# Compressed attention scores: from eight small matmuls in each query block to one set in each layer, turned per block

## The reference, cut to what matters

```python
k_c = rotary(compress(k_cmp, cmp_w1_k, cmp_w2_k), cmp_end, ROPE_DIM, ROPE_THETA)
v_c = compress(v_cmp, cmp_w1_v, cmp_w2_v)
mask_c = cmp_end[None, :] <= pos[:, None]
s_c = jnp.einsum('bsgjd,bngd->bgjsn', q, k_c)
p_c = masked_softmax(s_c, mask_c) * mask_c
o_cmp = jnp.einsum('bgjsn,bngd->bsgjd', p_c.astype(v_c.dtype), v_c)
...
o = g[..., 0:1] * o_cmp + g[..., 1:2] * o_slc + g[..., 2:3] * o_win
```

## Time and profile before

| | |
|---|---|
| median of 3 executions | 2146.18 us (2144.44 to 2149.34) |
| profiled execution, its own time | 2142.9 us |
| its span in the profile | 2141.1 us |
| PE busy | 2087.1 us, 97% of the span, 9868 instructions |
| DVE busy | 1229.9 us, 57% |
| ACT / POOL busy | 670.5 us / 918.6 us |
| granted TensorE clock, mean | 0.99 of full speed |

### The profile page before, as it was taken

One profiled execution on the slowest core, in us unless ns is written; L12 is line 12 of the kernel. 1 busy time (PEld: TensorE's weight loads), 2 busy tenths in 40 slices (PEclk: granted clock), 3 DMA queues, 4 the chain that ended last, 5 costly groups with the idle time before them and its releaser, 6 DMA issues.

```text
span 2141.1 us, 32149 instructions
## 1 busy us (share of the span) xinstructions
PE 2087.1 (97%) x9868; PEld 1646.9 (77%) x9868; DVE 1229.9 (57%) x1849; ACT 670.5 (31%) x977; POOL 918.6 (43%) x672
## 2 busy tenths in 40 slices
PE   8999999999999999999999999899999999999997
PEld 6766666788888788888877666668888887888886
DVE  8666767523235888872257668665223278888522
ACT  4244523333332322222223444223233322222222
POOL 3422224444445555545544222234444455555553
PEclk9999999999999999999999999999999999999998
DMA  5311123223232222223232111222322222222323
GB/s 195 104 58 40 50 64 99 80 97 98 98 98 92 96 93 94 97 91 118 95 116 93 50 43 48 82 84 86 102 94 97 98 99 89 98 98 93 107 98 108
DMA packets 57275, 194.90 MB, mean 91 GB/s; under 512 B 6880, under 2 KB 7392, under 8 KB 57056
## 3 DMA queue, kind: packets, MB, share of 16 engines
q1 hardware_dynamic: 52416, 186.14, 25.9%
q10 hardware_dynamic: 4768, 7.61, 1.3%
HBM read 186.64 MB, written 2.10 MB: 88 GB/s over the span
## 4 chain that ended last, share of the span: by engine, by line
PE 91%; DVE 6%; issue 2%; ACT 1%; DMA 0%; ACTq 0%; SPq 0%; DVEq 0%
PE acc L1150 27%; PE acc L1152 27%; PE acc L1151 26%; PE o L1334 2%; PE s L1308 2%; PE t L1316 2%; PE o L1368 1%; PE s L1295 1%; PE s L1358 1%; DVE win_k L752 1%; PE t L1345 0%; DMA w_raw<-weights_dram 0%; PE s L1384 0%; DVE rstd L724 0%; DVE y_lo L940 0%
## 5 line engine op out<-in xcount | busy, mean ns | idle before, releaser
L423 POOL TENSOR_TENSOR w_lo<-w_raw,w_hi 128x512 fp32r<-128x512 f32 x668 | 918.4, 1396 | 1197.9 <-ACT w_hi L445 1181.7
L1150 PE MATMUL acc<-xg_hi,w_hi 128*128 128x512 f32 x1904 | 778.1, 409 | 10.9 <-DVE kT L693 5.6
L1152 PE MATMUL acc<-xg_hi,w_lo 128*128 128x512 f32 x1904 | 747.7, 393 | 0.0
L1151 PE MATMUL acc<-xg_lo,w_hi 128*128 128x512 f32 x1904 | 745.7, 392 | 0.0
L445 ACT ACTIVATE w_hi<-w_raw 128x1024 fp32r<-128x1024 f32 x336 | 355.4, 1058 | 883.1 <-PE acc L1152 806.1
L1150 PEld LDWEIGHTS acc<-xg_hi,w_hi 128*128 128x128 f32 x1904 | 359.7, 189 | 117.3 <-issue 42.8
L1151 PEld LDWEIGHTS acc<-xg_lo,w_hi 128*128 128x128 f32 x1904 | 360.6, 189 | 76.7 <-issue 7.0
L1152 PEld LDWEIGHTS acc<-xg_hi,w_lo 128*128 128x128 f32 x1904 | 359.7, 189 | 77.6
L1027 DVE TENSOR_TENSOR work<-acc,rstd 128x512 f32<-128x512 f32 x64 | 44.1, 690 | 256.1 <-PE acc L1152 256.1
L1150 PE MATMUL acc<-act_hi,w_hi 128*128 128x512 f32 x352 | 136.9, 389 | 0.0
L1151 PE MATMUL acc<-act_lo,w_hi 128*128 128x512 f32 x352 | 136.9, 389 | 0.0
(11 more groups left out here) (199 smaller groups left out, 2257.6 us busy)
## 6 DMA issues: line engine op xcount, KB each, us to landing
w_raw<-weights_dram SPq DMA_DIRECT2D x339, 512.0 KB, 3.3
x<-xT_dram SPq DMA_DIRECT2D x8, 256.0 KB, 5.5
rot<-rq ACTq DMA_DIRECT2D x16, 128.0 KB
rot<-rk ACTq DMA_DIRECT2D x16, 128.0 KB
dec<-decay_dram ACTq DMA_DIRECT2D x8, 256.0 KB, 3.5
out_dram<-x SPq DMA_DIRECT2D x8, 256.0 KB, 2.3
con<-consts_dram SPq DMA_DIRECT2D x1, 1406.0 KB, 11.3
w1k<-w_dram SPq DMA_DIRECT2D x2, 512.0 KB, 8.7
```

Of the source, the lines that this page charges most:

```text
L423: nc.gpsimd.tensor_tensor(w_lo[:, slot, part], w_raw[:, slot, part], w_hi[:, slot, part].bitcast(F32), ALU.subtract).then_inc(lo_ready, 1)
L1150: mm(tile, w_h, right_hi, start=first, stop=False)
L1151: mm(tile, w_h, right_lo, start=False, stop=False)
L1152: return mm(tile, w_l, right_hi, start=False, stop=last)
```

## The change

1. `cmp_keys` (new, slot 3, once a layer): PE makes the scores of all 8 heads against all 512 queries, with keys on partitions. The stationary operand is a 64x32 piece of `kc`, padded from 31 to 32 keys with zeros; the moving operand is 64x512 of `qT`. Head `j` of group `g` writes partitions 32j to 32j+31 of the bank of group `g`. DVE copies both banks to `cmp_s`.
2. `cmp_scores` on PE is now two transposes of 128x128 from `cmp_s`, one for each group. In block 0 the three compressed steps stand one slot later (5, 7, 9).
3. `cmp_turn` on PE is two transposes of 128x128 in one bank, and DVE makes one copy of 256 columns. `cmp_pT` is double-buffered.
4. The compressed values are stored four times, each in its own 32 partitions of a zero-filled `vcz`, so that the product in `values` has 128 rows. To make them, PE runs 8 matmuls and not 2, and DVE 4 instructions and not 1. Three memsets are new at each layer's start.

```diff
-    if _n < UNITS and _n % 16 == 0:
+    if _n < UNITS and _n % 16 == (0 if _qi else 1):
         _e.append(("cmp_scores", _qi))
...
+SIDE[3] += [("cmp_keys", _g) for _g in range(KV_GROUPS)]
...
                 then(ve.memset(rot[:, :, :], 0.0))
+                ve.memset(vcz[:, :, :], 0.0).then_inc(chain, 1)
+                ve.memset(cmp_p[:, :, NCMP:32], 0.0).then_inc(chain, 1)
+                then.n += 2
+                then(ve.memset(kc[:, NCMP:32], 0.0))
...
-                s_end(ve.tensor_scalar(vc[0:NCMP, :], s_of("vc")[0:NCMP, 0:P], 0.5, None, ALU.mult), "vc")
+                for j in range(4):
+                    rows = slice(32 * j, 32 * j + NCMP)
+                    ins = ve.tensor_scalar(vcz[rows, j, :], s_of("vc")[rows, 0:P], 0.5, None, ALU.mult)
...
+                def cmp_keys(e):
+                    s_wait(e)
+                    s_end(ve.tensor_copy(cmp_s[:, e[1], :], s_of(e)[:, :]), e)
...
                 def cmp_turn(e):
-                    for half in range(2):
-                        t_wait((*e, half))
-                        if e[1]:
-                            dve.wait_ge(pv_done, pv_count(L, ("values", 16 * e[1] - 1)))
-                        t_end(ve.tensor_copy(cmp_pT[0:NCMP, half, :], t_of((*e, half))[0:NCMP, :]), (*e, half))
+                    t_wait(e)
+                    if e[1] >= 2:
+                        dve.wait_ge(pv_done, pv_count(L, ("values", 16 * e[1] - 17)))
+                    t_end(ve.tensor_copy(cmp_pT[:, e[1] % 2, :, :], t_of(e)[:, 0:KV_GROUPS * P].rearrange("p (g n) -> p g n", g=KV_GROUPS)), e)
...
+                            for j in range(4):
+                                ins = mm(b[32 * j:32 * j + NCMP, DH * i:DH * i + DH], hid[:, i * NCMP:(i + 1) * NCMP],
+                                         V("w2v", 0, DH)[0:DH, :], start=True, stop=True)
...
+                def cmp_keys(e):
...
+                    pe.wait_ge(v_made, v_count(L, "kc"))
+                    banks = [s_begin(("cmp_keys", g)) for g in range(KV_GROUPS)]
+                    alone(pe)
+                    for j in range(4):
+                        for g in range(KV_GROUPS):
+                            r = slice(64 * g, 64 * g + 64)
+                            ins = mm(banks[g][32 * j:32 * j + 32, :], kc[r, :], qT[r, j, :], start=True, stop=True)
...
                 def cmp_scores(e):
...
-                    for h in range(HEADS):
-                        r = slice(64 * (h // 4), 64 * (h // 4) + 64)
-                        ins = mm(b[:, 32 * h:32 * h + NCMP], qT[r, h % 4, qi * P:(qi + 1) * P], kc[r, 0:NCMP], start=True, stop=True)
-                        if h == 3:
-
-                            ins.then_inc(rows_done, 1)
-                            pe.wait_ge(rows_done, L * QT + (qi + 1))
+                    for g in range(KV_GROUPS):
+                        ins = nc.tensor.transpose(b[:, g * P:(g + 1) * P], cmp_s[:, g, qi * P:(qi + 1) * P], ident)
...
-                        products.append((vc[0:NCMP, :], cmp_pT[0:NCMP, :, j * P:(j + 1) * P]))
+                        products.append((vcz[:, j, :], cmp_pT[:, qi % 2, :, :]))
...
-                        for i in range(4):
-                            ins = nc.tensor.transpose(b[0:NCMP, i * P:(i + 1) * P], cmp_p[:, 4 * half + i, :], ident)
+                    for g in range(KV_GROUPS):
+                        ins = nc.tensor.transpose(b[:, g * P:(g + 1) * P], cmp_p[:, 4 * g:4 * g + 4, :].rearrange("p h n -> p (h n)"), ident)
```

More of the change, by code:

```diff
@@ L132 @@
 S_USES = ["sumsq1", "hid_k", "hid_v", "kc", "vc", "kc_swap"]
-S_USES += [_e for _e in SEQUENCE if _e[0] in ("gate", "cmp_scores", "scores", "ret_scores", "ret_var", "pool")]
+S_USES += [_e for _e in SEQUENCE if _e[0] in ("gate", "cmp_keys", "cmp_scores", "scores", "ret_scores", "ret_var", "pool")]
 S_USES += ["sumsq2"]
@@ L811, in _ @@
                 s_wait("vc")
-                s_end(ve.tensor_scalar(vc[0:NCMP, :], s_of("vc")[0:NCMP, 0:P], 0.5, None, ALU.mult), "vc")
+                for j in range(4):
+                    rows = slice(32 * j, 32 * j + NCMP)
+                    ins = ve.tensor_scalar(vcz[rows, j, :], s_of("vc")[rows, 0:P], 0.5, None, ALU.mult)
+                    if j < 3:
+                        ins.then_inc(chain, 1)
+                        then.n += 1
+                s_end(ins, "vc")
                 s_wait("kc_swap")
@@ L848, in cmp_scale @@
                     dve.wait_ge(a_made, a_count(L, ("cmp_scores", qi)))
-                    then(ve.tensor_reduce(c_den, cmp_p[:, :, :], AX.X, ALU.add))
+                    then(ve.tensor_reduce(c_den, cmp_real, AX.X, ALU.add))
                     gate_over_sum(qi, 0, c_den)
@@ L995, in mean @@
                               ("u", g), wait=True)
-                steps = {"gate": gate, "cmp_scores": cmp_scores, "scores": scores, "turn": turn, "values": values,
+                steps = {"gate": gate, "cmp_keys": cmp_keys, "cmp_scores": cmp_scores, "scores": scores, "turn": turn, "values": values,
                          "cmp_turn": cmp_turn, "cmp_scale": cmp_scale, "scale": scale, "ret_scores": ret_scores,
@@ L1340, in cmp_turn @@
                     pe.wait_ge(v_made, v_count(L, ("cmp_scale", e[1])))
-                    for half in range(2):
-                        b = t_begin((*e, half))
-                        last_wait()
-                        for i in range(4):
-                            ins = nc.tensor.transpose(b[0:NCMP, i * P:(i + 1) * P], cmp_p[:, 4 * half + i, :], ident)
-                        ins.then_inc(t_done, 1)
+                    b = t_begin(e)
+                    last_wait()
+                    for g in range(KV_GROUPS):
+                        ins = nc.tensor.transpose(b[:, g * P:(g + 1) * P], cmp_p[:, 4 * g:4 * g + 4, :].rearrange("p h n -> p (h n)"), ident)
+                    ins.then_inc(t_done, 1)
                 def ret_turn(e):
@@ L1474, in _ @@
             ins.then_inc(spread_ready, 1)
[L1478 removed]
+CHAIN_LAYER, CHAIN_J, CHAIN_F, CHAIN_D = 207, 4, 15, 2
 def _constants():
```

36 lines of the change are left out of this document (18 added, 18 removed).

## The result

The changed kernel takes 2120.39 us (median of 4 executions, 2118.66 to 2121.46), the kernel before beside it 2145.97 us (4 executions, 2144.44 to 2149.34): ratio 0.9883, with a 95% interval of 0.9871 to 0.9896. That is 25.6 us less, and 2120 was forecast. The profiled execution of the changed kernel took 2118.66 us, 24.2 less than the 2142.9 of before.

The account below looks back on a forecast made before the run. PE's instruction stream was taken as the bound (busy 97% of the span). The terms -14.3 - 5.2 - 4.8 + 2.3 + 0.2 + 0.5 - 5.0 = -26.3 us, applied to the 2146.2 us median, gave 2120 us, range 2112 to 2132.

Parts of the forecast that it names:

- scores: Compressed scores in the B stage: two transposes a block replace the score matmuls, 7.13 us gained a layer, 14.3 in both.
- turn: Turn of the probabilities in the B stage: two transposes instead of 8 gain 0.65 us, eight times, 5.2 us.
- product in `values`: Compressed product in `values`: 128 rows instead of 31 avoid a shape change, 0.15 us at 32 places, 4.8 us.
- keys: Eight key matmuls a layer: run side by side at a pair's cost, 1.16 us each layer, +2.3; bound +7.6.
- `vcz` matmuls on PE: 12 more of the smallest records a layer for `vcz`: side by side, 0.1 us a layer, +0.2; bounds 0 and 1.7.
- `vcz` instructions on DVE: Three further DVE instructions for `vcz`: fall into idle time ahead of a `take`, no cost.
- memsets: Three DVE memsets ahead of the reciprocal: hidden in the second layer, +0.5 us in the first, lengthening PE's wait for `kT`.
- clock: Granted clock at 0.50 after compressed scores: three of four falls gone as stretches shrink, 5.0 us gained; bounds 0 and 6.8.
- the rival that they go pair by pair: Key matmuls run as four pairs in a row, not all together: 5.3 us more, 2125 us; chance 0.15.
- the rival that had it late in all three: DVE late in all of blocks 1 to 3: 1.2 less in four places, 4.8 us, 2125 us; chance 0.2.
- Nothing was lost later: Answers a rival: gain lost to later PE waits for DVE at the retention part's rotated keys, 2146 us; chance 0.04.
- Slower, by the clock: Rival: transposes and keys count little as activity, so more clock falls, 1.7 us each; 2151 us at 15 more; chance 0.03.

Follow-up runs that it names:

- the last experiment on DVE's queue: Changed kernel with DVE's row sums and scaling of the compressed probabilities left out in block 3 (two one-column stand-ins for four instructions): 2118.16 us, ratio 0.9875.
- the version with later memsets: The spread version with the three memsets moved behind the reciprocal, ahead of the take of tile 7, nothing else: 2118.11 us, ratio 0.9879.
- the spread version: Changed kernel with compressed scores and scaling in slots 5 and 7 and the turn in slot 10, in all blocks: 2117.31 us, ratio 0.9872.
- the steps in slots 5, 7 and 9: Changed kernel with compressed scores, scaling and turn of blocks 1 to 3 also in slots 5, 7 and 9, as block 0 has them: 2121.09 us, ratio 0.9891.
- pairing alone, with a second bank: Kernel before, its eight score matmuls a block paired from both row halves, a bank per half, no wait between, mask in two DVE instructions: 2134.7 us, ratio 0.9955.

## Why the prediction was right

The terms, as forecast and as the two first profiles have them from main to main, both layers together:

| term | forecast | measured |
|---|---|---|
| scores | -14.3 | -13.9 |
| turn | -5.2 | -3.3 |
| product in `values` | -4.8 | -4.7 |
| keys | +2.3 | +2.2 |
| `vcz` matmuls on PE | +0.2 | +0.05 |
| `vcz` instructions on DVE | 0 | +0.8 |
| memsets | +0.5 | 0 to +0.2 |
| clock | -5.0 | -5.4, by difference |
| sum | -26.3 | -24.2 |

The clock's term is what the others leave of the 24.2 us. Counted by its stretches it would be more, 15.4 less 8.5 us, so 6.8; some of those of before lie where PE had little to do (the start, and the end of layer 0's attention).

The medians fell by 25.6 us, 1.4 more than the profiled executions. That the median came within half a microsecond of the 2120 that was forecast is in part luck: the terms other than the clock gave 18.8 us of the 21.3 that were forecast, and the clock's term and the scatter of the executions made up for it.

- **Bound.** Right: PE's stream was the bound and stayed it, and the gain stands in the two attention stages and nowhere else.
- **Scores.** Right. Per layer 2.64 + 1.92 + 0.48 + 1.92 us, against 2.63 + 1.90 + 0.7 + 1.90. The third block was a little worse than forecast, since DVE's mask comes 1.11 us late.
- **Turn.** Mechanism right, size wrong, the largest miss. "With 0.22 the gain is 0.65, eight times" took one slot for all eight. In blocks 0 to 2 the slot gained 0.54, 0.61 and 0.61 us. In block 3 it lost 0.10: there the two transposes wait for DVE's 512-column copies, and the last experiment on DVE's queue shows that what DVE is spared comes off this slot one to one. Reading, a slot of block 0, could not show this. The trace of before had it: in block 3 the slot was 3.17 us long, not the 0.87 + 1.39 = 2.26 that the earlier trace rows give, and PE waited 0.56 us in it for the same copies. What six transposes fewer save there, the longer wait takes back. Also, had shown that DVE gets short of time in the later blocks, and the forecast used that for the scores and not for the turn, four slots on.
- **Product.** Right, and shown by undoing it: 4.6 us. The steps between the records show the change of shape as the cause.
- **Keys.** Right by the pair's row, 1.35 us for eight; the rival that they go pair by pair asked for 4.0, and a further pair costs 0.84 us only where it stands on the same place. The Trainium skill ("TensorE: Matmul & The Clock Gate", What overlaps and what doesn't / Measured speedup) has packed tiles cost one matmul plus about 4 ns for each further one; the trace agrees, with 1.35 us for eight and 1.39 for a pair.
- **Small additions.** The sum of them was right, 0.7 forecast and 0.9 to 1.1 measured, and the parts were not. "The three further DVE instructions for `vcz` fall into idle time ahead of a `take`" failed: they are 0.97 us long, the idle time ahead of that take was 0.82, and PE waits for just this take, in both layers. The memsets, which were costed, hardly cost anything, and PE's wait for `kT` stayed at 5.6 us in all, where 0.5 more was named as a sign.
- **Clock.** The size came out, the reason only in part. The forecast counted falls at four places of one profile as if they belonged to them. They don't: a second profile of each program has some of them elsewhere, and more of them in the changed kernel. Half of the half-clock time differs between the kernels by 2 to 12 us over the four pairings of profiles, so a single pair could have missed the forecast's 5.0 either way. Why a given stretch falls stays open, and the length of the wait does not decide it. In the fourth block eight of ten longer waits have a fall behind them (1.93 to 3.17 us, five variants, two layers) and none of 0.56 to 1.41 us has. But in the version with later memsets the clock stays at 1.00 in the first layer behind the very wait of 2.23 us that the spread version has:

```profile
233.95 0.44 PE L1369 MATMUL t<-con,cmp_p 128*128 128x128 f32 x2 [2.23 <-DVE pT L896]
234.32 1.16 PE L1331 MATMUL s<-kT,qT 64*128 64x512 f32 x4
```

With the steps in slots 5, 7 and 9, the wait of 3.17 us has a fall behind it in the first layer and none in the second. And both profiles of the changed kernel have a fall behind block 2, where the wait is 1.1.
- **Rivals.** DVE's wait did take a place, above all in the turn, with 1.9 us less gain than forecast there. For the mask of the scores DVE was late in the third block alone, so the rival that had it late in all three is out. Nothing was lost later: PE's six waits in the retention part for the rotated keys `rk` add up to 14.6 us, 14.8 before. *Slower, by the clock* did not come either: with transposes in the scores' stretches too, the clock was at half for less time.

## What to carry to other kernels

What helped small matmuls here was to put them side by side on different rows and columns of the array, and to pad them to the shape of their neighbours: pairing alone, with a second bank, gave 10 us and padding 4.6. Cost a step that recurs in each block in the last block too, and go by DVE's idle time there: where its queue was full, moving PE's step to another slot only moved the wait. Count the instructions ahead of each result that PE waits for, even the smallest: three of 0.3 us on DVE cost 0.4 us a layer here, more than a memset of 512 columns did.

## What the runs showed of the hardware

- Eight f32 matmuls of 64x512 on eight places of the array (two row halves, four column groups) held the main matmuls apart for 1.35 us, a pair of them 1.39 us; each further pair on one of the same places cost 0.84 us.
- Four records of 31 rows between others of 128 rows cost 0.145 us more than with 128 rows: the step to a pair of another shape was 0.21 us and the next 0.16, where steps within one shape were 0.11.
- Two executions of one program have the granted clock at 0.50 at different places, for 31 and 41 us in all, and the times of the two profiled executions, 2142.9 and 2149.0 us, differ by 6.1 us; half of the difference in half-clock time is 5.1.
